# Sparse attention one unit deeper: four score buffers, value products of four heads at once, and a later wait in the output product

## What is computed

```python
def dsa_mixer(x, w_in, kv_norm_g, kidx_ln_g, kidx_ln_b, w_out, rel_bias):
...
    def block_fn(args):
        qb, qib, wb, blk = args
        t = blk * Q_BLOCK + jnp.arange(Q_BLOCK)
        s_idx = jnp.einsum('bthd,bsd->bths', qib, k_idx,
                           preferred_element_type=jnp.float32) * (IDX_DIM ** -0.5)
...
        causal = key_pos[None, :] <= t[:, None]
        score = jnp.where(causal[None], score, -jnp.inf)
        _, sel = lax.top_k(score, topk)
...
        kv_sel = jax.vmap(lambda c, i: c[i])(c_kv, sel)
        logits = jnp.einsum('bthc,btjc->bthj', qb, kv_sel,
                            preferred_element_type=jnp.float32) * (KV_LATENT ** -0.5)
        bucket = t5_bucket(jnp.maximum(t[None, :, None] - sel, 0))
        bias = jnp.moveaxis(rel_bias[bucket], -1, 2)
        logits = logits + bias.astype(jnp.float32)
        logits = jnp.where(valid[:, :, None, :], logits, -jnp.inf)
        p = jax.nn.softmax(logits, axis=-1).astype(x.dtype)
        o = jnp.einsum('bthj,btjc->bthc', p, kv_sel)
        return o.reshape(Bsz, Q_BLOCK, hq)

    o = lax.map(block_fn, (to_blocks(q), to_blocks(q_idx), to_blocks(w_idx), jnp.arange(nb)))
    o = jnp.moveaxis(o, 0, 1).reshape(Bsz, S, hq)
    return o @ w_out
```

## Time and profile before

| | us |
|---|---|
| median of 3 runs (lowest, highest) | 2935.92 (2935.75, 2938.6) |
| the profiled execution | 2935.28 |
| its span in the profile | 2933.5 |
| attention stage, first logits to last output copy | 2117.9 to 2235.2 |
| output product `dsa_out`, first to last product | 2242.1 to 2339.9 |
| PE busy, share of the span | 2618.0, 89% |
| mean granted PE clock, share of 2.4 GHz | 0.976 |

### The profile page before, as it was taken

How to read it: one execution, slowest core, us unless ns; L and a number is a source line. 1 busy time by engine, 2 the same in 40 slices (tenths; PEclk the granted TensorE clock), 3 DMA queues, 4 the chain that set the end, 5 groups by cost and what they waited for, 6 DMA issues and landing times.

```text
span 2933.5 us, 51406 instructions
## 1 busy us (share of the span) xinstructions
PE 2618.0 (89%) x21069; PEld 2105.9 (72%) x21069; DVE 1150.6 (39%) x2123; ACT 751.7 (26%) x1254; POOL 196.1 (7%) x217
## 2 busy tenths in 40 slices
PE   6999999999899999998987778899998978777787
PEld 5888887777688888776666666676777766666666
DVE  4655645533542244445411111155865441111114
ACT  3222333264332234223200000023375330000001
POOL 0100002000000000001000000202000011000002
PEclk8999999999999999998999999999999989999999
DMA  7655423313222322222399999942310129999993
GB/s 245 198 173 185 164 79 99 98 58 115 86 87 86 100 94 94 81 78 87 154 422 422 422 422 422 419 136 88 109 46 29 45 103 409 422 422 422 422 422 138
DMA packets 206771, 594.38 MB, mean 203 GB/s; under 512 B 9472, under 2 KB 133584, under 8 KB 157264
## 3 DMA queue, kind: packets, MB, share of 16 engines
q1 hardware_dynamic: 202880, 575.47, 51.0%
q0 software_dynamic: 3504, 16.63, 1.8%
q10 hardware_dynamic: 288, 0.89, 0.1%
HBM read 590.79 MB, written 7.41 MB: 204 GB/s over the span
## 4 chain that ended last, share of the span: by engine, by line
PE 66%; DMA 22%; DVE 6%; ACT 2%; issue 2%; SPq 1%; DVEq 0%; ACTq 0%
PE bank L1870 37%; DMA ring<-in_exp_w 21%; PE bank L2228 9%; PE bank L1960 5%; PE bank L2192 2%; PE bank L2296 2%; PE bank L2132 1%; PE bank L2435 1%; PE bank L2327 1%; DVE ring_low L1174 1%; SPq L547 1%; DMA ring<-in_w_ada 1%; PE bank L2403 1%; PE bank L2053 1%; PE bank L2426 1%
## 5 line engine op out<-in xcount | busy, mean ns | idle before, releaser
L1870 PE MATMUL bank<-parts 128*128 128x512 f32 x2624 | 817.8, 393 | 22.5 <-DVE parts L1180 10.3
L2228 PE MATMUL bank<-ring,arena 128*64 128x256 f32 x4096 | 493.3, 391 | 174.5 <-DMA ring<-in_exp_w 174.5
L1870 PEld LDWEIGHTS bank<-parts 128*128 128x128 f32 x2624 | 493.7, 189 | 125.0 <-issue 22.2
L2228 PEld LDWEIGHTS bank<-ring,arena 128*64 128x64 f32 x4096 | 326.9, 135 | 304.9 <-issue 193.9
L1870 PE MATMUL bank<-parts,ring_low 128*128 128x512 f32 x1312 | 513.6, 391 | 0.0
L1174 DVE TENSOR_TENSOR ring_low<-ring,parts 128x2048 fp32r<-128x2048 f32 x106 | 238.2, 2251 | 212.4 <-ACT parts L771 212.1
L1622 DVE SCALAR_TENSOR_TENSOR arena<-arena,bank 128x128 f32<-128x128 f32 x128 | 44.3, 346 | 650.0 <-ACT arena L917 650.0
L1870 PEld LDWEIGHTS bank<-parts,ring_low 128*128 128x128 f32 x1312 | 247.9, 189 | 52.2
L2246 PEld LDWEIGHTS bank<-arena,ring 128*64 128x64 f32 x8192 | 265.7, 138 | 18.1 <-ACT arena L749 3.3
L771 ACT ACTIVATE parts<-ring 128x2048 fp32r<-128x2048 f32 x106 | 198.9, 1877 | 283.6 <-DMA ring<-in_w_ffn_in 107.2
L2246 PE MATMUL bank<-arena,ring 128*64 128x64 f32 x8192 | 263.4, 222 | 2.2 <-ACT arena L749 2.2
(11 more groups left out here) (335 smaller groups left out, 2838.2 us busy)
## 6 DMA issues: line engine op xcount, KB each, us to landing
ring<-in_exp_w SPq DMA_DIRECT2D x384, 1024.0 KB, 10.3
ring<-in_w_ffn_in SPq DMA_DIRECT2D x44, 1024.0 KB, 6.7
ring<-in_w_ada SPq DMA_DIRECT2D x36, 1024.0 KB, 5.2
ring<-in_w_ffn_out SPq DMA_DIRECT2D x20, 1024.0 KB, 5.0
ring<-in_w_in SPq DMA_DIRECT2D x18, 1024.0 KB, 5.1
ring<-in_conv_w_in SPq DMA_DIRECT2D x12, 1024.0 KB, 5.2
ring<-in_attn_w_in SPq DMA_DIRECT2D x10, 1024.0 KB, 5.3
ring<-in_attn_w_out SPq DMA_DIRECT2D x8, 1024.0 KB, 9.9
```

The source lines that it names most:

```text
L1870: i = mm(o, a[:, cols[0], cols[1]], b, start=first_ and n == 0, stop=last_ and n == 2)
L2228: x = mm(bank[s][64 * f:64 * f + 64, 0:2 * P].rearrange("p (w n) -> p w n", w=2), XW[:, s, k], ring[:, 3 * s:3 * s + 2, c0:c0 + 2 * P - 1: ...
```

## The change

- `S2` has four score buffers instead of three (`PT2`, which lay behind it, is gone), and the chain is one unit deeper: the transposes and their copies are those of unit i - 3.
- The transposed tiles go to `PT4`, which lies in the buffer `U` (idle in this stage) and holds two groups of four heads. The copies write there in runs of 128 columns with a stride of 512 (`probs`).
- The value products are those of a group g of four heads at once: qb + 1 products of 512 columns, one in each PE iteration from 4g + 7 on, and one output copy of 128 x 512 for the group (`given_at`). PE waits for the copies of the group's last two units ahead of its first product.
- `token_output` waits for its last chunk only when token tile 0 has come to it.

```diff
@@ -151,6 +151,7 @@
             pass
         SEL = sb("picked", [P, TT, PAIRS], F32R)
         ROWS = U[:].rearrange("p k s -> p (k s)").rearrange("p (v d) -> p v d", v=4)
+        PT4 = U[:].rearrange("p k s -> p (k s)").rearrange("p (g j n) -> p g j n", g=2, j=TT)
         keep = sb("keep", [P, N_KEEP])
         par = sb("par", [P, N_PARAM])
         mod = sb("mod", [P, 72])
@@ -298,8 +299,7 @@
         KI = area(20992, TT, P)
         KIT = area(21504, SEQ)
         IR = area(22016, 2, SEQ)
-        S2 = area(23040, 3, SEQ)
-        PT2 = area(24576, 2, SEQ)
+        S2 = area(23040, 4, SEQ)
         MASK = rounded(18944, 3, SEQ)
         CAUSAL = rounded(20480, 1, P)
         IDENT = rounded(20608, 1, P)
@@ -319,6 +319,15 @@
 
         def query_bank(h):
             return bank[2 + h] if h < 2 else bank[4 + h % 4]
+
+        def probs(u):
+
+            qb, h = u // HEADS2, u % HEADS2
+            return PT4[:, u // 4 % 2, 0:qb + 1, P * (h % 4):P * (h % 4) + P]
+
+        def given_at(i):
+
+            return [g for g in range(16) if 4 * g + 7 + g // 4 == i]
 
         def turned_banks(j, t):
 
@@ -1080,29 +1089,29 @@
                     weights_high(split_at["dsa_q"] + h // 2 + 1)
                 query(h)
             units = [(qb, h) for qb in range(TT) for h in range(HEADS2)]
-            for i in range(len(units) + 2):
+            for i in range(len(units) + 3):
                 if i < len(units):
                     n = (units[i][0] + 1) * P
                     act.wait_ge(sem("att_max"), ATT["max"] + i + 1)
-                    A_(S2[:, i % 3, 0:n], S2[:, i % 3, 0:n], ACT.Exp, scale=-1.0, bias=DS[:, i:i + 1],
+                    A_(S2[:, i % 4, 0:n], S2[:, i % 4, 0:n], ACT.Exp, scale=-1.0, bias=DS[:, i:i + 1],
                        accum_out=DS[:, 64 + i:65 + i]).then_inc(sem("att_e"), 1)
                 if 0 <= i - 1 < len(units):
                     u = i - 1
                     n = (units[u][0] + 1) * P
                     act.wait_ge(sem("att_ri"), ATT["ri"] + u + 1)
-                    A_(S2[:, u % 3, 0:n], S2[:, u % 3, 0:n], ACT.Copy, scale=DS[:, 128 + u:129 + u])\
+                    A_(S2[:, u % 4, 0:n], S2[:, u % 4, 0:n], ACT.Copy, scale=DS[:, 128 + u:129 + u])\
                         .then_inc(sem("att_p"), 1)
-                if i >= 2:
-                    u = i - 2
+                if i >= 3:
+                    u = i - 3
                     n = (units[u][0] + 1) * P
                     if u % 2 == 0:
                         act.wait_ge(sem("att_tp"), ATT["tp"] + u + 1)
-                        if u:
-                            act.wait_ge(sem("att_pv"), ATT["pv"] + u - 1)
-                    if u % 2 == 0:
-                        A_(PT2[:, 0, 0:n], bank[2][:, 0:n], ACT.Copy).then_inc(sem("att_pt"), 1)
-
-            act.wait_ge(sem("att_y"), ATT["y"] + 64)
+                        if u >= 8:
+                            act.wait_ge(sem("att_pv"), ATT["pv"] + u // 4 - 1)
+                        A_(probs(u), bank[2][:, 0:n].rearrange("p (j q) -> p j q", q=P), ACT.Copy)\
+                            .then_inc(sem("att_pt"), 1)
+
+            act.wait_ge(sem("att_y"), ATT["y"] + 16)
             out_high("dsa_out", HEADS2, lambda k: Q2[:, k], UP, lambda k: None)
             layer_norm(2)
             moe(1)
@@ -1768,33 +1777,33 @@
             units = [(qb, h) for qb in range(TT) for h in range(HEADS2)]
             dve.wait_ge(sem("bias_dma"), 80)
 
-            for i in range(len(units) + 3):
+            for i in range(len(units) + 8):
                 if i < len(units):
                     qb, h = units[i]
                     n = (qb + 1) * P
-                    S = S2[:, i % 3, 0:n]
+                    S = S2[:, i % 4, 0:n]
                     dve.wait_ge(sem("att_mm"), ATT["mm"] + i + 1)
-                    if i >= 3:
-                        dve.wait_ge(sem("att_tp"), ATT["tp"] + i - 2)
+                    if i >= 4:
+                        dve.wait_ge(sem("att_tp"), ATT["tp"] + i - 3)
                     nc.vector.tensor_tensor_reduce(S, bank[i % 2][:, 0:n], TOE[:, h, SEQ - n:SEQ], 1.0, 3.0e38,
                                                    ALU.add, ALU.min, DS[:, i:i + 1]).then_inc(sem("att_max"), 1)
                 if 0 <= i - 1 < len(units):
                     u = i - 1
                     dve.wait_ge(sem("att_e"), ATT["e"] + u + 1)
                     nc.vector.reciprocal(DS[:, 128 + u:129 + u], DS[:, 64 + u:65 + u]).then_inc(sem("att_ri"), 1)
-                if i >= 2 and i % 2:
-                    u = i - 2
+                if i >= 3 and i % 2 == 0 and i - 3 < len(units):
+                    u = i - 3
                     n = (units[u][0] + 1) * P
                     dve.wait_ge(sem("att_tp"), ATT["tp"] + u + 1)
-                    if u >= 2:
-                        dve.wait_ge(sem("att_pv"), ATT["pv"] + u - 1)
-                    nc.vector.tensor_copy(PT2[:, 1, 0:n], bank[3][:, 0:n]).then_inc(sem("turned_odd"), 1)
-                if i >= 3:
-                    u = i - 3
-                    qb, h = units[u]
-                    dve.wait_ge(sem("att_pv"), ATT["pv"] + u + 1)
-                    nc.vector.tensor_copy(Q2[:, h, qb * P:qb * P + P], bank[4 + u % 2][:, 0:P])\
-                        .then_inc(sem("att_y"), 1)
+                    if u >= 8:
+                        dve.wait_ge(sem("att_pv"), ATT["pv"] + u // 4 - 1)
+                    nc.vector.tensor_copy(probs(u), bank[3][:, 0:n].rearrange("p (j q) -> p j q", q=P))\
+                        .then_inc(sem("turned_odd"), 1)
+                for g in given_at(i - 1):
+                    qb, h = units[4 * g]
+                    dve.wait_ge(sem("att_pv"), ATT["pv"] + g + 1)
+                    nc.vector.tensor_copy(Q2[:, h:h + 4, qb * P:qb * P + P],
+                                          bank[4 + g % 2][:].rearrange("p (h q) -> p h q", h=4)).then_inc(sem("att_y"), 1)
             dve.wait_ge(sem("resid"), 8)
             out_low("dsa_out", HEADS2, lambda k: Q2[:, k], UP, lambda: deep_out("dsa_out", 4, 2, 0), half_at=6)
             layer_norm(2, lambda t: deep_out("dsa_out", 4, 2, 1, (t,)))
@@ -1971,10 +1980,10 @@
                         for t in range(TT):
                             last = product(half, c, k, t)
                     last.then_inc(sem(name + "_used"), 1)
-                for c in (n - 2, n - 1):
-                    ready(1, c)
                 for t in range(TT):
                     for c in (n - 2, n - 1):
+                        if t == 0:
+                            ready(1, c)
                         for k in range(4 * c, 4 * c + 4):
                             last = product(1, c, k, t)
                         if t == TT - 1:
@@ -2414,28 +2423,29 @@
                 else:
                     pe.wait_ge(sem("att_pt"), ATT["pt"] + u // 2 + 1)
 
-            for i in range(len(units) + 3):
+            for i in range(len(units) + 7):
                 if i < len(units):
                     logits(i)
-                if 0 <= i - 2 < len(units):
-                    u = i - 2
+                if 0 <= i - 3 < len(units):
+                    u = i - 3
                     pe.wait_ge(sem("att_p"), ATT["p"] + u + 1)
                     if u >= 2:
                         turned(u - 2)
                     for j in range(units[u][0] + 1):
-                        x = tp(bank[2 + u % 2][:, P * j:P * j + P], S2[:, u % 3, P * j:P * j + P], ident)
+                        x = tp(bank[2 + u % 2][:, P * j:P * j + P], S2[:, u % 4, P * j:P * j + P], ident)
                     x.then_inc(sem("att_tp"), 1)
-                if i >= 3:
-                    u = i - 3
-                    qb = units[u][0]
-                    turned(u)
-                    if u >= 2:
-                        pe.wait_ge(sem("att_y"), ATT["y"] + u - 1)
-                    for j in range(qb + 1):
-                        x = mm(bank[4 + u % 2][:, 0:P], CKV[:, j], PT2[:, u % 2, P * j:P * j + P],
-                               start=(j == 0), stop=(j == qb))
-                    x.then_inc(sem("att_pv"), 1)
-            pe.wait_ge(sem("att_y"), ATT["y"] + 64)
+                g, j = (i - 7) // 4, (i - 7) % 4
+                if i >= 7 and g < 16 and j <= units[4 * g][0]:
+                    qb = units[4 * g][0]
+                    if j == 0:
+                        turned(4 * g + 2)
+                        turned(4 * g + 3)
+                        if g >= 2:
+                            pe.wait_ge(sem("att_y"), ATT["y"] + g - 1)
+                    x = mm(bank[4 + g % 2][:], CKV[:, j], PT4[:, g % 2, j], start=(j == 0), stop=(j == qb))
+                    if j == qb:
+                        x.then_inc(sem("att_pv"), 1)
+            pe.wait_ge(sem("att_y"), ATT["y"] + 16)
             token_output("dsa_out", HEADS2, UP, lambda t: turn_tokens(2, t), lambda t: logits_of(1, t))
             moe(1)
 
```

## The result

| | before | changed |
|---|---|---|
| median of 5 runs, us | 2938.60 | 2924.03 |
| lowest, highest | 2935.75, 2943.13 | 2922.20, 2929.07 |
| profiled execution, span | 2935.28, 2933.5 | 2929.07, 2927.2 |

The ratio is 0.995 (95% interval 0.9939 to 0.996), so the change makes the kernel about 14.6 us faster (by the medians), where 33.8 were forecast: 2924.03 us for the predicted 2901.5, and above the range of 2896 to 2915. The changed kernel's profiled execution is 5.0 us above its median, and its attention stage starts 6.4 us later than the profile's of before (2124.3 for 2117.9), ahead of everything that the change touches. So lengths are compared here, not positions.

A forecast was written before the change was run, and what follows sets the result against it. PE, nearly gapless in the attention stage, was taken to be held by a two-unit loop through ACT's scaling. Gains of 29.4 (stage), 2.7 and 1.65 (output product) made 33.8 us off 2935.28: 2901.5, range 2896 to 2915.

The forecast's parts named there:

- the first of the attention stage: Attention stage, query block 3: value-product pair of 512 columns takes 0.46 us for 0.99, so PE's work is 1.64 a unit.
- then stands for 0.46 until ACT's scaling is done: Attention stage, block 3 before the change: PE pauses 0.46 us a unit ahead of the transposes, in a two-unit loop of 4.98.
- The sign of being wrong that the prediction gave for its loops: Attention stage: loops are wrong if block 3 takes over 1.8 us a unit at clock 1.00, ACT idle before its Exp.
- the loop of three units that the prediction had: Attention stage, block 3: transposes wait for ACT's copy of two units before; 4.88 us over three units, 1.63 a unit.
- ACT's busy time as the bound of the stage: Attention stage: ACT's busy time plus a little for starts sets each block, 80.7 us for 112.0, a gain of 31.3.
- The end of the stage: From last logits to ACT's next work: 8.6 to 8.9 us for 7.8; 1.9 taken off the gain, leaving 29.4.
- The output product: Last chunk: PE's stand falls from 3.34 us to 0.6 to 0.8, gaining 2.7, plus 1.65 for the clock; together 4.35.
- that rival: Attention stage: copies in runs of 128 columns cost double on ACT, 13.3 us come back, kernel 2914.8; chance 0.08.
- The swinging clock: Attention stage: PE spends half the time at either clock level, stage 93.7 us, kernel 2914.5; chance 0.05.
- The rivals' times at half clock: Attention stage at 1.2 GHz: 2.56 us a block 3 unit; throughout, about 2927, chance 0.03; with pause, about 2954, chance 0.04.
- The added wait ahead of a group: Attention stage: PE's wait for DVE's copy before a group's first value product costs nothing, with 0.2 us of cover.
- the chain stays bound, and only the shorter products count: Attention stage: an overlooked wait keeps the chain at two units; shorter value products gain 10.7 us, about 2922; chance 0.04.

The follow-up runs named there:

- e9_narrow_later: Kernel before with the chain one unit deeper, four score buffers and 128-column value products two units behind the transposes, old output-product wait; ratio 0.9948 to before.
- e1_wait_split: Kernel before with only the split wait of the output product in `token_output`; ratio 0.9982 to before.

## Why the prediction was wrong

**The step that failed** is the first of the attention stage: "The value products become one of 512 columns a unit in two passes. Such a pair takes 0.46 us (the logits' own row), where the eight short passes take 0.99." A fp32 pass of 512 columns keeps PE for 0.43 us, and the pair for 0.86. The price stands twice in "PE's work is then 0.46 + 0.23 + 0.49 + 0.46 = 1.64 us a unit", for the logits and for the value product. With 0.86 in both places, and 0.44 for the transposes, it is 2.39, which is what the units of the changed kernel take. The 0.46 was taken from the distance between the starts of L2403 and L2404 in the earlier trace rows. Behind a fp32 pair this trace puts the next start about 0.4 early; the distance to the start after that (L2426) is 1.09, and I explained the missing part as a pause. The rule of reading that stands with the times before, from one start to the next, does not hold for this row. The parts so read add up to 2.63 us in a unit of 2.49, which could have been a sign. The chain in order of time had it right, in the kernel before:

```profile
2202.64 0.86 PE bank L2403 x2
2203.50 0.23 PE bank L2404
2203.74 0.48 PE bank L2426 x4
2204.22 0.98 PE bank L2435 x8
2205.20 0.86 PE bank L2403 x2
```

Logits 0.86, mask 0.23, transposes 0.48, value products 0.98, and no wait of 0.2 us or more between. In the changed kernel, in the same view:

```profile
2205.86 0.86 PE bank L2445 x2
2206.72 0.86 PE bank L2412 x2
2207.82 0.44 PE bank L2435 x4
2208.25 0.86 PE bank L2445 x2
```

**The pause that was none.** "then stands for 0.46 until ACT's scaling is done" rests on the row of the weight loads (PEld). The waits of the kernel before in block 3:

```profile
ACT arena L1087 <- DVE arena L1779: 13.5, 17, 1.4
DVE arena L1779 <- PE bank L2404: 12.8, 16, 0.8
PEld bank L2426 <- ACT arena L1093: 6.6, 16, 0.7
DVE arena L1796 <- PE bank L2435: 4.4, 10, 0.6
PEld bank L2404 <- issue: 3.8, 16, 0.2
```

PEld waited for ACT for 6.6 us, and the view names no wait of PE. The weight loader's idle time lay under the mask product, nearly all of it: the units take 2.43 and 2.56 us in turn, and 2.42 all of them once the value products come later (e9_narrow_later). So what the loop cost in block 3 is at most 0.13 us in every second unit, and not 0.46 in each. PE's busy time of 39.3 out of 39.4 us said so as well, and I had put it aside as modelled. So block 3 was bound by PE before and stayed so: 2.49 to 2.39 us a unit, not to 1.66. Half the columns took 0.43 off it and more work on ACT added nothing. The sign of being wrong that the prediction gave for its loops came true: over 1.8 us at clock 1.00, with ACT idle before its Exp.

The Trainium skill has the rule ("FP8 and Floating Point Precision", "TensorE Precision Notes"): a true fp32 product takes four passes through the array. Four times 512 columns at 2.4 GHz, with about one column a clock as the single-pass mask product shows it (0.23 us for 512), are 0.853 us, an estimate from that page, and the traces' 0.86 agrees. It speaks against widening these products for PE's sake, and the prediction did not weigh it.

**The loops.** Blocks 0 to 2 did have a loop over two units through ACT's scaling, and the change does remove it. But it has a twin through ACT's copy, which I had at three units for the transposes and overlooked for the value products: with depth alone it binds at two. The changed order escapes it since a group's product comes later. What is left are waits of the transposes for ACT, of 2.6 us in block 0 and 1.8 in block 1, of which 1.7 and 1.8 are for its copy (L1111), as in the loop of three units that the prediction had. In blocks 1 and 2 the change gained 3.7 and 4.6 us, where 6.6 and 9.6 were forecast. There too the price is what was missing: with products of 16 columns these blocks take 16.8 and 21.3 us, under the 17.7 and 22.2 forecast. ACT's busy time as the bound of the stage was not tested in block 3, where PE was the longer in every run.

**The rest of the sum.** The end of the stage was to cost 8.9 us behind the last logits and costs 11.3: the last group's four products at 0.86 and not 0.46 are 1.6 of that, and the product ahead of the last transposes is on the chain too. The output product was to gain 4.35 us: its stand shrank by 2.7 and the clock held, as forecast, and the first products behind the stage took about 0.9 more, being at half clock for 5.5 us instead of 3.6. The stand before them, 7.6 us for 7.2, does not explain that: in e1_wait_split it is 7.2, and they are at half clock for 5.6. The 1.65 for the clock behind the old wait is one execution's figure; the traces have 0 to 3. The copies in runs of 128 columns cost what they did before (0.57 us on ACT), so that rival falls. The swinging clock falls too: 1.00 in all four windows. The argument against it rested in part on pauses of 0.46 us that PE did not have in block 3; but waits of PE of up to 0.7 us in blocks 0 and 1 of the kernel before left the clock at 1.00 as well. What brought it to 0.50 for 3.4 us in block 0 of two other traces is open. The rivals' times at half clock took every column at one clock, which makes 1.28 us of a unit of block 3 at 2.4 GHz; the traces have 2.39, so those rivals were priced at about half. The added wait ahead of a group cost nothing: no wait of PE at L2445 is in the view. Of the rivals, "the chain stays bound, and only the shorter products count", at 2922, came nearest, for the wrong reason: the chain came loose and the products were not shorter.

## What to carry to other kernels

Price a matmul by what PE does until the instruction after next, in the chain or by two starts on, and by type: in these traces 512 columns cost 0.43 us for each of two passes in fp32 and 0.23 in fp32r, so that wider products of the same columns save only the weight loads' share (0.03 us of 0.89 here). And put a corrected price in wherever the same kind of row was priced: here the logits carried the error as well as the product that was changed. An idle weight loader is not an idle PE; ask the waits of PE itself before a pause is put into a loop. When a step is moved one iteration later to open a loop, look for the next wait on the same in-order engine: depth was worth nothing until the value products, too, came after the copy they need.

## What was not expected of the hardware

- In a fp32 pair the two passes of 512 columns stood 0.43 us apart, and the next matmul's start was recorded 0.46 us after the pair's first one, while its work began at 0.86.
- Eight fp32 passes of 128 columns with a weight load each took 0.89 us, nearly nothing more than the two of 512 (0.86): the loads are nearly covered by the fp32 passes.
- A fp32 product of 16 columns, two passes with their loads, cost 0.22 us in a unit (1.75 for 1.53), about as much as one fp32r pass of 512 (0.23).
- A stand of 0.63 us was followed by no fall of the granted clock in any trace. One of 3.34 us was followed by 3.3 us of products at 0.50 in the kernel before, by 6.1 us in two other traces and by none in e9_narrow_later.
